# Decoder step on one core: two blocks of the most used expert's tokens are computed early, between the router's steps

## The reference

```python
xp = xp + g1p * mix_merge(att, cv, w_out[l])                  # mixer's projection and gated residual
def moe(h, w_router, b_router, wg, wu, wd):                   # 16 experts in 4 groups
    logits = t @ w_router;  probs = softmax(logits);  sel = probs + b_router
    best = argmax over groups of the sum of a group's two highest sel
    idx  = the two highest sel within that group              # two experts for each token
    w    = p_sel / sum(p_sel)
    a = t @ wg[e];  b = t @ wu[e];  act = silu(a) * b * gate  # 1024 -> 512, for the chosen e
    return act @ wd[e], summed over both experts              # 512 -> 1024
xp = xp + g2 * moe(modulate(rmsnorm(xp)))
```

## Time and profile before

| | us |
|---|---|
| median of 3 runs | 1234.73 |
| lowest and highest run | 1234.27, 1238.36 |
| profiled execution, first to last instruction | 1233.3 |
| PE busy in it | 1154.7 |
| DVE busy | 600.7 |
| ACT busy, POOL busy | 336.7, 254.3 |

### The profile page before, as it was taken

How to read it: one execution, slowest core, us unless ns; L and a number is a source line. 1 busy time by engine, 2 the same in 40 slices (tenths; PEclk the granted TensorE clock), 3 DMA queues, 4 the chain that set the end, 5 groups by cost and what they waited for, 6 DMA issues and landing times.

```text
span 1233.3 us, 19314 instructions
## 1 busy us (share of the span) xinstructions
PE 1154.7 (94%) x6769; PEld 540.8 (44%) x6769; DVE 600.7 (49%) x1161; ACT 336.7 (27%) x713; POOL 254.3 (21%) x312
## 2 busy tenths in 40 slices
PE   6999999999989899998999966999999999999996
PEld 4444444444446666665444433333333333333332
DVE  0010867786779999997965357111211211212212
ACT  2132221222138888887212221000000000000000
POOL 2011101221049600000100001123222222232322
PEclk9999999999999999999999986999999999999998
DMA  9843333322347465645833246996789878976663
GB/s 359 332 144 103 103 103 107 97 88 86 90 155 259 142 210 170 205 138 210 311 117 110 91 150 237 375 380 244 262 283 326 312 243 281 367 233 240 219 221 119
DMA packets 115859, 253.37 MB, mean 205 GB/s; under 512 B 15054, under 2 KB 29518, under 8 KB 114760
## 3 DMA queue, kind: packets, MB, share of 16 engines
q1 hardware_dynamic: 94241, 208.42, 48.6%
q0 software_dynamic: 17568, 39.35, 9.1%
q10 hardware_dynamic: 3984, 4.72, 1.1%
HBM read 399.77 MB, written 39.22 MB: 356 GB/s over the span
## 4 chain that ended last, share of the span: by engine, by line
PE 83%; DMA 5%; ACT 4%; issue 4%; DVE 3%; SPq 0%; ACTq 0%; POOL 0%; POOLq 0%; DVEq 0%
PE bank L1784 20%; PE bank L1461 20%; PE bank L1798 10%; PE bank L1652 8%; PE bank L1441 3%; PE bank L1495 2%; PE bank L1535 2%; PE bank L1545 2%; PE bank L1523 2%; PE bank L1774 2%; PE bank L1316 1%; DMA big<-in_w_up_dram 1%; DMA big<-in_w_down_dram 1%; PE bank L1558 1%; ACT mid L1123 1%
## 5 line engine op out<-in xcount | busy, mean ns | idle before, releaser
L1784 PE MATMUL bank<-big,mid 128*64 128x512 f32 x1232 | 283.1, 600 | 2.2 <-DMA big<-in_w_up_dram 1.7
L1461 PE MATMUL bank<-big 128*128 128x512 f32 x560 | 249.2, 598 | 0.1
L1461 PEld LDWEIGHTS bank<-big 128*128 128x128 f32 x560 | 103.7, 190 | 131.2 <-issue 131.2
L1784 PEld LDWEIGHTS bank<-big,mid 128*64 128x64 f32 x1232 | 87.1, 138 | 161.4 <-issue 160.5
L1957 DVE SCALAR_TENSOR_TENSOR cvT<-low,cw,cvT 128x256 f32<-128x256 f32 x360 | 156.9, 510 | 0.0
L1798 PE MATMUL bank<-big,mid 128*64 128x512 f32 x608 | 133.8, 592 | 1.2 <-DMA big<-in_w_down_dram 1.2
L2062 DVE TENSOR_TENSOR_SCAN big<-big 128x513 f32<-128x513 f32 (+4 forms) x96 | 90.2, 978 | 8.2 <-ACT big L1090 8.1
L2485 DVE TENSOR_TENSOR xt<-xt,bank 128x512 f32<-128x512 f32 x20 | 13.8, 688 | 148.5 <-ACT xt L1258 148.5
L2504 DVE TENSOR_TENSOR mid<-bank,low 128x512 f32<-128x512 f32 x38 | 24.5, 686 | 120.0 <-PE bank L1798 79.9
L1798 PEld LDWEIGHTS bank<-big,mid 128*64 128x64 f32 x608 | 44.0, 137 | 87.8 <-issue 87.8
L800 POOL TENSOR_TENSOR st<-st,mhalf 128x16 f32<-128x16 f32 (+1 forms) x9 | 25.2, 2801 | 252.6 <-DVE st L1988 243.9
(11 more groups left out here) (341 smaller groups left out, 1349.7 us busy)
## 6 DMA issues: line engine op xcount, KB each, us to landing
big<-in_w_gate_dram SPq DMA_DIRECT2D x42, 2048.0 KB
big<-in_w_up_dram SPq DMA_DIRECT2D x41, 2048.0 KB
big<-in_w_down_dram SPq DMA_DIRECT2D x41, 2048.0 KB
low<-in_w_ada_dram SPq DMA_DIRECT2D x32, 512.0 KB, 4.2
low<-in_cache_v_dram SPq DMA_DIRECT2D x64, 256.0 KB
big<-in_w_in_dram SPq DMA_DIRECT2D x8, 1280.0 KB, 17.1
xt<-in_x_prompt_dram SPq DMA_DIRECT2D x16, 512.0 KB, 4.7
mid<-in_w_ada_dram SPq DMA_DIRECT2D x8, 1024.0 KB, 13.9
```

Of the source, the lines that this page charges most:

```text
L1461: mm = pe.matmul(bank[:, 4 if cc == 2 else cc, :], hT[:, s, k, :], w_in_sb[:, k, cc * 512:(cc + 1) * 512], start=(k == 0), stop=(k == KD - 1))
L1784: mm = pe.matmul(bank[half, 2 * s + w, :], xgT[:, s, k, half], moving, start=(k == 0), stop=(k == KD - 1))
```

## The change

In the mixing loop, after the first four tiles (`NBT` = 4) have their logits, DVE chooses their experts (`early_logits`, `early_choice`), PE counts their ranks (`early_ranks`), and DVE finds the expert with the most rows among these 512 tokens (`early_expert`) and places up to 256 of its rows in two blocks of 128 (`early_places`, `early_slots`, `early_rows_of_slots`). SP then loads that expert's three matrices into the lower slots in place of expert 0's, POOL gathers the rows, and PE computes both blocks with full 128-row matmuls. The blocks' pieces stand between the router's and the routing's steps on PE. The ranks of the main routing start with two more matmuls (`shift_used`, `shift_gone`) that take the rows served early out of the count. The spare gate matrix of expert 1 and the preload of expert 0 are gone.

By the counts above, 224 rows of expert 15 are served early and 236 stay: 4 units instead of 8, 36 units in all, so cut is 18 and there are 18 passes. The lower half then walks through 0 1 2 3 3 4 4 5 5 5 6 6 6 7 8 8 9 9 and the upper through 10 10 11, 12 six times, 13 twice, 14 three times, 15 four times. Both halves get a new expert at passes 2, 3 and 14.

The diff, cut to what is spoken of later:

```diff
-            sp.wait_ge(S["pv_mm"], U)
-            for w_sb, w_d in ((wg_sb, w_gate), (wu_sb, w_up), (wd_sb, w_down)):
-                sp.dma_start(w_sb[:, 0, :, :], w_d[0, 0].rearrange("(k p) n -> p k n", p=P)).then_inc(S["first_in"], 16)
+            def load_early_expert():
+                sp.wait_ge(S["pv_mm"], U)
+                sp.wait_ge(S["e_sel"], N0["e_sel"] + 1)
+                e = sp.value_load(early_exp[0:1, 0:1], min_val=0, max_val=E - 1)
+                for w_sb, w_d, landed in zip((wg_sb, wu_sb, wd_sb), (w_gate, w_up, w_down), e_w_in):
+                    sp.dma_start(w_sb[:, 0, :, :], w_d[0, bass.ds(e, 1), :, :].rearrange("a (k p) n -> p (a k) n", p=P))\
+                        .then_inc(landed, 16)
+
             for t in range(NT):
                 if t + 2 < NT:
                     load_x2(t + 2)
+                if t == NBT + 2:
+                    load_early_expert()
                 store_x1(t)
                 store_h2(t)
-            sp.wait_ge(S["mix_mm"], N0["mix_mm"] + NT)
-            sp.dma_start(wg_spare, w_gate[0, 1].rearrange("(k p) n -> p k n", p=P)).then_inc(S["spare_in"], 16)
             for landed, n0 in zip(x1_st, X1_ST0):
                 sp.wait_ge(landed, n0 + 16 * (NT // 3))
             sp.wait_ge(h2_stored[0], 16 * 5)
             sp.wait_ge(h2_stored[1], 16 * 4)
-            sp.wait_ge(S["first_in"], N0["first_in"] + 48)
+            sp.dma_start(gate_row[:, 0, :], bass.AP(g2_d.tensor, 0, [[0, P], [1, D]])).then_inc(S["e_grow_in"], 16)
+            sp.wait_ge(S["e_gu"], N0["e_gu"] + NEB)
+            sp.dma_start(wg_sb[:, 0, :, :], w_gate[0, 0].rearrange("(k p) n -> p k n", p=P)).then_inc(S["first_in"], 16)
...
             e0, = pass_experts(zero_exp, 0, 1)
+            sp.wait_ge(S["first_in"], N0["first_in"] + 16)
+            sp.wait_ge(S["e_gu"], N0["e_gu"] + 2 * NEB)
             load_w(wg_sb, w_gate, wg_in, e0, (0, None))
-            sp.wait_ge(xg_in[0], 16)
-            load_w(wu_sb, w_up, wu_in, e0, (0, None))
-            load_w(wd_sb, w_down, wd_in, e0, (0, None))
+            load_w(wu_sb, w_up, wu_in, e0, (None, None))
             sp.wait_ge(S["tiles_ready"], 2)
             e1, e2 = pass_experts(first_exp, 1, 2)
...
+            sp.wait_ge(S["e_y"], N0["e_y"] + 2 * NEB)
+            load_w(wd_sb, w_down, wd_in, e0, (None, None))
...
+            load_w(wg_sb, w_gate, wg_in, e1, e0)
...
             for t in range(NT):
                 pool.wait_ge(S["x2_var"], N0["x2_var"] + t + 1)
                 pool.tensor_tensor(st[:, 2:3], st[:, 0:1], mhalf[:, 0:1], ALU.pow).then_inc(S["x2_rstd"], 1)
+                if t == NBT + 2:
+                    pool.wait_ge(S["e_col"], N0["e_col"] + 1)
+                    pool.wait_ge(S["ln_done"], N0["ln_done"] + 3)
+                    pool.wait_ge(h2_stored[0], 16 * (NBT // 2))
+                    pool.wait_ge(h2_stored[1], 16 * (NBT // 2))
+                    for s in range(NEB):
+                        pool.indirect_dma_start(out=xe[:, s, :], out_offset=None, in_=h2_d[0:NBT * P, :],
+                                                in_offset=rows_at(ex_col[:, s:s + 1])).then_inc(xg_in[s], EARLY)
...
+            pool.wait_ge(S["tok_ready"], 1)
...
+            for s in range(NEB):
+                pool.wait_ge(S["e_done"], N0["e_done"] + s + 1)
+                pool.indirect_dma_start(out=yp, out_offset=rows_at(eo_col[:, s:s + 1]), in_=ye[:, s, :], in_offset=None,
+                                        bounds_check=SEQ - 1, **FAR).then_inc(out_st[s], EARLY)
...
-                if t == NTP - 2:
-                    square(NTP - 1)
-                    square(NTP)
+                if t == NBT + 2:
+                    act.wait_ge(S["e_hot"], N0["e_hot"] + 1)
+                    nc.scalar.activation(b_at32, b_at, ACT.Copy).then_inc(S["e_hot32"], 1)
...
+                if t == NTP - 2:
+                    square(NTP - 1)
+                    for s in range(NEB):
+                        evac_xe(s)
+                    square(NTP)
...
             act.wait_ge(S["z_ready"], N0["z_ready"] + 1)
             nc.scalar.activation(r_e, r_z, ACT.Exp).then_inc(S["exp_ready"], 1)
+            for s in range(NEB):
+                early_sigmoid(s)
             act.wait_ge(S["hot_ready"], N0["hot_ready"] + 1)
             nc.scalar.activation(at_row32, at_row, ACT.Copy).then_inc(S["row32_ready"], 1)
+            evac_acte(0)
...
+            def early_turn(s):
+                pe.wait_ge(xg_in[s], EARLY)
+                if s == 0:
+                    pe.wait_ge(S["x1_tmp"], N0["x1_tmp"] + NTP)
+                for k in range(KD):
+                    mm = pe.transpose(bank[:, XE_BANKS[s][k // 4], (k % 4) * P:(k % 4 + 1) * P],
+                                      xe[:, s, k * P:(k + 1) * P], identf[:, :])
+                mm.then_inc(S["e_xps"], 1)
+
+            def early_gate_or_up(s, w, k0, k1):
+                if w == 0 and k0 == 0:
+                    pe.wait_ge(S["e_xsb"], N0["e_xsb"] + 2 * s + 2)
+                if w == 1 and s == 1 and k0 == 0:
+                    pe.wait_ge(S["h2T_sb"], 2 * NT)
+                if k0 == 0:
+                    pe.wait_ge(e_w_in[w], E_W0 + 16)
+                for k in range(k0, k1):
+                    mm = pe.matmul(bank[:, (EG_BANK, EU_BANK)[w][s], :], xeT[:, s, k, :], (wg_sb, wu_sb)[w][:, 0, k, :],
+                                   start=(k == 0), stop=(k == KD - 1))
+                if k1 == KD:
+                    mm.then_inc(S["e_gu"], 1)
+
...
+            def early_down(s, w):
+                pe.wait_ge(S["e_asb"], N0["e_asb"] + s + 1)
+                pe.wait_ge(e_w_in[2], E_W0 + 16)
...
                 if t == NTP - 2:
+                    early_slots()
                     mix_sample()
...
-                if t + 2 < NTP:
...
                     mix(t + 2, 0)
+                if t + 2 == NTP - 1:
+                    mix(t + 2, 0, (0,))
+                    mix(t + 2, 0, (1,), (0, 2))
+                    early_ranks()
+                    mix(t + 2, 0, (1,), (2, 4))
...
                 if t == NTP - 1:
+                    early_gate_or_up(0, 0, 0, KD // 2)
                     row_sum()
                 if 1 <= t < NTP:
                     router_strips(t - 1)
                 route(t)
                 if 1 <= t < NTP:
                     router_sum(t - 1)
+                if t == NTP - 2:
+                    early_turn(0)
+                    early_turn(1)
+                if t == NTP - 1:
+                    early_gate_or_up(0, 0, KD // 2, KD)
             for t in range(NTP - 1, NT):
                 router_strips(t)
                 router_sum(t)
+            early_gate_or_up(1, 0, 0, KD)
...
-            pe.matmul(ranks, before[:, :], r_maskb, start=True, stop=False)
+            pe.matmul(ranks, identb[:, :], shift_used.rearrange("p t e -> p (t e)"), start=True, stop=False)
+            pe.matmul(ranks[:, 0:NBT * E], identb[:, :], shift_gone.rearrange("p t e -> p (t e)"), start=False, stop=False)
+            pe.matmul(ranks, before[:, :], r_maskb, start=False, stop=False)
...
+            early_gate_or_up(0, 1, 0, KD)
             pe.wait_ge(S["hot_ready"], N0["hot_ready"] + 1)
             to_slots(bank[:, 1, 0:2 * NG].rearrange("p (w n) -> p w n", w=2), at_row,
                      lambda a: first_id[:, a, 0:2, :], NG)
-            pe.wait_ge(S["hot_ready"], N0["hot_ready"] + 2)
-            pe.wait_ge(S["row32_ready"], N0["row32_ready"] + 1)
-            to_slots(bank[:, 3, 0:MT].unsqueeze(1), at_row32, lambda a: tile_w[:, a, :].unsqueeze(1), MT)
+            early_gate_or_up(1, 1, 0, KD // 2)
+            early_turn_act(0)
+            early_gate_or_up(1, 1, KD // 2, KD)
+            early_down(0, 0)
+            early_turn_act(1)
+            early_down(0, 1)
+            pe.wait_ge(S["tok_ready"], 1)
+            early_down(1, 0)
+            early_down(1, 1)
...
             turn_x(0)
+            pe.wait_ge(S["hot_ready"], N0["hot_ready"] + 2)
+            pe.wait_ge(S["row32_ready"], N0["row32_ready"] + 1)
+            to_slots(bank[:, 3, 0:MT].unsqueeze(1), at_row32, lambda a: tile_w[:, a, :].unsqueeze(1), MT)
...
-            pe.wait_ge(S["first_in"], N0["first_in"] + 48)
+            pe.wait_ge(S["e_done"], N0["e_done"] + NEB)
             arrived(wg_in, 16)
             gate_or_up(0, 0, 0, KD)
...
             for t in range(NT):
                 normed(t)
+                if t == NBT + 1:
+                    early_expert()
+                if t == NBT + 2:
+                    early_rows_of_slots()
                 if t + 1 < NTP:
                     merged(t + 1)
+                if t == NBT + 1:
+                    early_places()
                 for j, at in LN_AT.items():
                     if t == at:
                         ln_center(j, 7)
@@ -2258,21 +2588,15 @@
                         ln_eps(j)
                         ln_diag(j)
                         ln_scale(j)
-                    if t == at + 2:
```

(5 more changed lines are left out.)

300 lines of the change are left out of this document (260 added, 40 removed).

## The result

The changed kernel takes 1250.57 us (median of 4 runs, 1249.51 to 1250.96); the kernel before, on the same chip, 1236.55. The ratio is 1.0116, 95% interval 1.0095 to 1.0137. The prediction was 1246.4 with a range of 1227 to 1259: slower, as forecast, by 14.0 us where I had 11.7. The profiled execution spans 1249.1 us. Profiles of the same instructions differ too: six of the experiments leave the early part as it is here, and in these seven profiles PE's wait for the gathered rows is 4.3 to 5.9 us, and the first pass's gate product, gate(0), starts between 791.5 and 793.5.

A forecast was written before the change was run, and what follows sets the result against it. Passes were taken as PE-bound at 22.51 us, the restart as load-bound: up(3) at 896.8 plus 14 passes gives 1211.9; with 4, 1.7 and 27.4, 1245.0; median 1.4 higher, 1246.4 us, range 1227 to 1259.

The forecast's parts named there:

- PE's work: Whole kernel: two passes removed save 45.0 us, early blocks add 47.5 us, so PE's work grows by 2.5 us.
- If only PE counted: Whole span without load waits: it would end at 1210, 23 us faster.
- Part 1: Mixing loop to the last logits: early work adds 15 us, including 5.5 waiting for gathered rows; logits at 747.6.
- Part 2: Routing after the last logits: mask at 756.3, early up of block 1 done at 773.5, gate(0) at 793.
- Part 3: Weight loads from 773.5 to up(3): 18 loads plus rows, 46.7 MB at 385 GB/s, so up(3) starts at 896.8.
- restart: First passes, gate(1) to up(3): waiting for loads costs 29 us against 867.6 on PE alone.
- Pass 14: Pass new in both halves right behind one with one new: 4 us of wait, bounds 1.7 to 8.
- Sum: Whole span: up(3) start, 14 passes, pass 14, lower clock and last pass total 1245.0; median 1.4 over it.
- A: Loads keep up: up(3) before 885, at most 1212 us, or partly 1220 to 1231; chance 0.17.
- B: Comes out even: no early wait for rows, less waiting at passes 3 and 14; 1231 to 1238; chance 0.12.
- D: No pass saved because the early expert is not expert 15: 20 passes, 45 us more, 1290; chance 0.02.
- C: Early part later still, gather and tile 6's store 6 us late behind the 6.3 MB load: 1252 to 1260; chance 0.12.

The follow-up runs named there:

- first experiment: Changed kernel with pass 0's upper-half up and down matrices loaded once the pass's experts are known, not behind the early products: 1246.39 us, ratio 1.0099.
- all together: Changed kernel, early turns and gate behind the last router sums, tile 6's stores before early weights, pass 0's three upper matrices loaded early: 1247.35 us, ratio 1.0111.
- halves: Changed kernel with every weight refill in two halves, pass 0's upper matrices still loaded behind the early products: 1235.72 us, ratio 0.9999 to the kernel before.

## Why the prediction was right

- **PE's work.** Predicted to grow by 2.5 us, measured 3.2, 1157.9 against 1154.7. Rows at a lower clock count as busy in both; with the loads left out it is 1151.4 against 1150.0. "If only PE counted", 1210: 1209.0 with the loads left out, the middle of two runs 9 us apart.
- **Part 1.** Last logits at 747.6 predicted, 747.8 measured; the wait for rows 5.5, measured 5.01. The choice of 5.5 us for it, between bounds of 0 and 9.6, was right. That the logits were hit to 0.2 us is luck: in the seven profiles with this early part they come between 747.7 and 749.7. The turns behind the wait take 3.7 to 4.0 us, lower clock included, where 2.2 and 1.7 for the clock were put in.
- **Part 2.** Mask 756.3 (756.55), early up ending at 773.5 (773.0), gate(0) at 793 (791.6). One assumption of the bounds holds one way only: that part 1's delay shifts all that follows ("all of it shifts 773.5"). Logits 8 us earlier gave 0.7 at gate(0).
- **Part 3.** up(3) at 896.8, measured 895.95; restart 29 us, measured 28.9. The sum was right and its picture wrong in one sentence: "the queue could also run dry; it does so for 1 or 2 us at most". From 800 to 830 the engines moved 312 instead of 385 GB/s, 5.7 us lost, and there are two queues with a slot's release between them. From 830 to 885 the engines were faster than 385, 1.5 us gained, and in the last 12 us slower, 2.6 us lost. It was made up for by the bytes: the windows from 775 to 897 hold 44.3 MB (385 x 25 + 312 x 30 + 392 x 30 + 399 x 25, and 302 GB/s over the last 12), where I had 46.7, 6.2 us at 385. The size of the restart was thus right partly by chance, and the first experiment's expectation, built on the picture, missed.
- **Pass 14.** This is the term that was mis-sized: 4 us, with 1.7 for the clock, and measured 1.59 + 5.75 and 2.3 of clock, 9.6. The mechanism was right, the price was set with only the 1.74 us of an isolated double pass to go by the earlier trace rows; the waits came to 7.3, inside the bounds of 1.7 to 8. By the working used for part 3 it could have been had: from the release of the gate slots at 1114.84 to up(14) at 1151.37 are 36.5 us; five loads and the rows are 10.5 + 3.3 MB, 36 us at 385 GB/s, and PE covers 29.5. Leaving pass 13's loads out takes 4.4 us off the wait before up(14), and the lower clock behind it with it.
- **Sum.** From up(3) to the last pass 4.6 us more than predicted, the start 0.9 less, the end (27.7 us instead of 27.4) 0.3 more: 1245.0 becomes 1249.1, and the median stands 1.5 over it.
- **Rivals.** *A* needed up(3) before 885: it came at 896. *B* needed no wait for the rows and less at pass 14; neither came. *D* fell with the 18 passes. *C* had the mechanism right (I had tile 6's store landed at 736; it was 744), but it cost nothing, since PE's turn of the sample tile stood behind the early gate product until 745.2. The kernel with the turns late shows its price without that cover, 8 to 10 us. The Trainium skill's rule on it ("DMA: Bandwidth & Descriptors", Queues, rings and completion order), that descriptors are consumed in ring order, agrees with the 16 us here and the missing wait with the stores in front. On the rate, the 399 GB/s of the window from 860 to 885 lie between its 358, the share of one of two busy cores, and its 425 for one alone (section Bandwidth).

Left open: whether another order of the queue (down before gate) would shorten passes 2 and 3; it wasn't tried. A change of the pairing, so that both halves never turn to a new expert together, wasn't tried either.

## What to carry to other kernels

Work put into an idle engine's gap can take away the buffers in which the next stage's data would have waited; list what was prefetched in the gap, and count the bytes from the moment the buffers come free to the moment PE needs the last of them, each release for itself. A buffer that is reused in place is worth splitting in halves before any more compute is moved. Where an engine waits for a late input, check whether its own total work would not end just as late.

## What the runs showed of the hardware that was not expected

- SP itself is held up while it issues. In saturated stretches the issue of two 2048 KB loads took 8.57, 8.10 and 12.46 us, against 0.5 to 1.7 for most pairs elsewhere (3.58 at 1129.80, and 4.39 for the two behind the second early up product). The third load of the early expert took 4.59. The small stores behind it were issued late as well: that of tile 6 to `h2_d` at 727.82, and with the stores in front at 723.95.
- A load of 2.10 MB took 10.7 us from its slot's release to the product even with little in front of it, twice the 5.4 us that its bytes take at 392 GB/s. In these 10.7 us the engines moved 3.0 MB, the gathers of rows among them, and hardly anything in the first 2 us (all together).
- Each of the changed kernel's four waits for weights over 5 us is followed by 1.5 to 2.3 us lost at a lower clock, so such a wait costs a quarter to 40% more than its length; in the other kernels it is up to 2.9 us. Behind shorter waits it goes either way: the 16 records behind 3.19 us (first experiment) took 3.65, behind 3.12 (all together) 6.54, and behind 2.35 (halves) 5.35.
